# Two of twenty-four weight slices per pair of expert blocks multiplied unsplit in a mixture-of-experts layer on one Trainium2 core

## What is computed

```python
def expert_block(args):
    xe, e = args
    gu = xe @ w_gu[e] + b_gu[e]
    gate = jnp.minimum(gu[..., 0::2], SWIGLU_LIMIT)
    up = jnp.clip(gu[..., 1::2], -SWIGLU_LIMIT, SWIGLU_LIMIT)
    act = (up + 1.0) * (gate * jax.nn.sigmoid(gate * SWIGLU_ALPHA))
    return act @ w_dn[e] + b_dn[e]
```

## Time and profile before

| | |
|---|---|
| median of 3 runs | 1439.85 us |
| the three runs | 1437.68, 1439.9, 1439.85 us |
| profiled execution, its own time | 1438.17 us |
| its span in the trace | 1436.5 us |
| mean granted TensorE clock | 0.989 of full |
| DMA moved | 472.82 MB, mean 329 GB/s |

### The profile page before, as it was taken

How to read it: one execution, slowest core, us unless ns; L and a number is a source line. 1 busy time by engine, 2 the same in 40 slices (tenths; PEclk the granted TensorE clock), 3 DMA queues, 4 the chain that set the end, 5 groups by cost and what they waited for, 6 DMA issues and landing times.

```text
span 1436.5 us, 20084 instructions
## 1 busy us (share of the span) xinstructions
PE 1333.8 (93%) x6418; PEld 1058.0 (74%) x6418; DVE 1282.2 (89%) x1252; ACT 1029.2 (72%) x941; POOL 426.8 (30%) x282
## 2 busy tenths in 40 slices
PE   6999989889999999999999899999999999999996
PEld 5876866776777777777877777777777777788883
DVE  7348565789999999999999999999999999999998
ACT  5344444537788888878787888888887878877772
POOL 0000000024343536243443335343535434311100
PEclk9999999899999999999999999999999999999998
DMA  9411130279999999999999999999999999999994
GB/s 353 159 60 59 34 147 16 77 262 385 398 399 401 400 390 398 406 392 403 400 406 394 397 394 398 394 391 405 399 400 397 404 394 395 391 378 377 368 371 178
DMA packets 102341, 472.82 MB, mean 329 GB/s; under 512 B 16499, under 2 KB 16539, under 8 KB 68000
## 3 DMA queue, kind: packets, MB, share of 16 engines
q1 hardware_dynamic: 87632, 451.79, 79.6%
q0 software_dynamic: 14672, 20.53, 4.1%
HBM read 467.78 MB, written 22.02 MB: 341 GB/s over the span
## 4 chain that ended last, share of the span: by engine, by line
PE 44%; DVE 24%; issue 14%; DMA 9%; ACT 8%; DVEq 0%; SPq 0%; ACTq 0%
DVE w_lo L991 13%; PE gu_bank L1529 9%; PE gu_bank L1531 9%; PE gu_bank L1530 9%; DMA raw<-in_w_down_dram 8%; ACT w_hi L639 6%; DVE arena L1373 2%; PE turn_bank L1529 2%; PE turn_bank L1531 2%; PE turn_bank L1530 2%; PE bank L1529 2%; DVE arena L1383 1%; ACT turned L815 1%; PE bank L1531 1%; PE bank L1530 1%
## 5 line engine op out<-in xcount | busy, mean ns | idle before, releaser
L991 DVE TENSOR_TENSOR w_lo<-raw,w_hi 128x2048 fp32r<-128x2048 f32 x411 | 921.5, 2284 | 69.6 <-ACT w_hi L639 68.6
L639 ACT ACTIVATE w_hi<-raw 128x2048 fp32r<-128x2048 f32 x411 | 776.4, 1919 | 131.7 <-PE gu_bank L1531 98.9
L601 POOL DMA_INDIRECT expert_rows<-arena x32 | 222.4, 6949 | 331.4 <-ACT arena L840 172.3
L1529 PE MATMUL gu_bank<-w_hi,turned 128*128 128x512 f32 x632 | 251.9, 399 | 12.3 <-DVE w_lo L991 8.3
L1531 PE MATMUL gu_bank<-w_hi,turned 128*128 128x512 f32 x632 | 247.0, 391 | 0.0
L1530 PE MATMUL gu_bank<-w_lo,turned 128*128 128x512 f32 x632 | 247.0, 391 | 0.0
L1535 PE MATMUL gu_bank<-w_hi,turned 128*128 128x512 f32 x448 | 179.9, 402 | 29.6 <-DVE w_lo L991 28.2
L1536 PE MATMUL gu_bank<-w_lo,turned 128*128 128x512 f32 x448 | 175.1, 391 | 0.0
L1529 PEld LDWEIGHTS gu_bank<-w_hi,turned 128*128 128x128 f32 x632 | 119.0, 188 | 47.6 <-DVE w_lo L991 16.9
L1531 PEld LDWEIGHTS gu_bank<-w_hi,turned 128*128 128x128 f32 x632 | 119.0, 188 | 25.4
L1530 PEld LDWEIGHTS gu_bank<-w_lo,turned 128*128 128x128 f32 x632 | 119.1, 188 | 23.2
(11 more groups left out here) (339 smaller groups left out, 1766.6 us busy)
## 6 DMA issues: line engine op xcount, KB each, us to landing
raw<-in_w_gate_up_dram SPq DMA_DIRECT2D x264, 1024.0 KB, 11.2
raw<-in_w_down_dram SPq DMA_DIRECT2D x132, 1024.0 KB, 9.1
raw<-in_w_in_dram SPq DMA_DIRECT2D x10, 1024.0 KB, 8.3
raw<-in_w_out_dram SPq DMA_DIRECT2D x4, 1024.0 KB, 6.1
raw<-expert_rows SPq DMA_DIRECT2D x4, 1024.0 KB, 6.6
raw<-in_w_mem_kv_dram SPq DMA_DIRECT2D x2, 1024.0 KB, 12.3
arena<-in_x_dram SPq DMA_DIRECT2D x1, 2048.0 KB, 13.8
arena<-in_position_tables_dram SPq DMA_DIRECT2D x1, 2048.0 KB, 17.5
```

The costliest lines, as they stand in the source:

```text
L601: pool.indirect_dma_start(y_dram, bass.IndirectOffsetOnAxis(idx_scatter, 0), y_row, None, bounds_check=TOPK * S - 1, oob_is_err=False).the ...
L639: a.activation(home, raw_ap, ACT.Copy).then_inc(hi_ready, 1)
L991: v.tensor_tensor(home[1], raw_ap, home[0].bitcast(F32), ALU.subtract).then_inc(lo_ready, 1)
L1529: pe.matmul(bank, a[0], b[0], start=first, stop=False)
```

## The change

In each of the 14 pairs two slices are no longer split: slice 5 of gate_up of the wide block behind a narrow one, and slice 0 of the down product of the wide block, which PE does in the following narrow block's section. Both are loaded to a buffer of their own (`spare`) and multiplied as plain float32, four matmuls each, with unsplit copies of the rows or activations that ACT keeps (`keep_x`, `keep_act`). They have no `hi` and no `lo`; the counts of the slice before are raised by two. SP signals the slot they would have had (`skip_slot`). The load of the down slice stands two places earlier in SP's order, behind k5 of the narrow block; that of the gate_up slice two places later, behind k7 of the wide block.

Slices 4 to 7 of block 0 are multiplied in plain float32 too, directly from the raw slots, and have no `hi` or `lo`; the rows for them are one unsplit copy by ACT (`x_first`), and turn_x(1) of block 0 is gone from DVE. The low part of the first half of block 0's rows is made on DVE after L1275 instead of after L1296.

The biases are loaded, split and saved during the projections (on DVE before lo_a(7)), the first block takes its bias rows from DRAM as the others do, and ones and the shifted identity are built by ACT. The last two slices before the attention ends are split two steps earlier on ACT, and on DVE at the start of a step. The loads of the final gain and the down biases move on POOL from the start of the blocks to after block 29's step.

The core of the diff (SP, PE, and the order on ACT and DVE in a pair):

```diff
+            def skip_slot(i, free):
+
+                sp.wait_ge(lo_ready, free)
+                sp.sem_inc(raw_in[i % 6], 16)
...
+            def narrow_after_wide(b, first=False):
+
+                before, e = experts_of(b)
+                for k in range(GU):
+                    if first and 2 <= k < 2 + GU - FIRST_WHOLE:
+                        sp.wait_ge(half_used, 19 + k)
+                    gate_up(e, k, GU + k, b * 12 + (7 + k))
+                    if k == 5:
+                        sp.wait_ge(half_used, b * 12 + 6)
+                        sp.dma_start(spare.rearrange("p (k n) -> p k n", k=2),
+                                     dn_dram[bass.ds(before, 1), :, 2 * WHOLE_DN:2 * WHOLE_DN + 2, :]
+                                     .rearrange("e p k n -> p (e k) n")).then_inc(whole_dn_in, 16)
+                for j in range(DN):
+                    if j == WHOLE_DN:
+                        skip_slot(2 * GU + j, b * 12 + (7 + GU + j))
+                    else:
+                        down(before, j, 2 * GU + j, b * 12 + (7 + GU + j))
+
+            def wide_after_narrow(b):
+
+                before, e = experts_of(b)
+                for k in range(GU):
+                    if k == WHOLE_GU:
+                        skip_slot(GU + k, b * 12 + (7 + k))
+                    else:
+                        gate_up(e, k, GU + k, b * 12 + (7 + k))
+                sp.wait_ge(half_used, b * 12 + (1 + GU + WHOLE_DN))
+                sp.dma_start(spare.rearrange("p (e n) -> p e n", e=1),
+                             gu_dram[bass.ds(e, 1), :, WHOLE_GU, :].rearrange("e p n -> p e n")).then_inc(whole_gu_in, 16)
+                for j in range(DN):
+                    down(before, j, 2 * GU + j, b * 12 + (7 + GU + j))
...
+            def gate_up_whole(n):
+
+                pe.wait_ge(whole_gu_in, n * 16)
+                for c in range(4):
+                    ins = pe.matmul(psum[c], x_whole, spare[:, c * 512:(c + 1) * 512], start=False, stop=False)
+                ins.then_inc(half_used, 1)
+
+            def down_whole(n):
+
+                pe.wait_ge(whole_dn_in, n * 16)
+                for kk in range(2):
+                    for c in range(2):
+                        at0 = kk * D + c * 512
+                        ins = pe.matmul(psum[4 + c], act_whole[:, kk * P:(kk + 1) * P], spare[:, at0:at0 + 512],
+                                        start=kk == 0, stop=False)
+                ins.then_inc(half_used, 1)
...
-                for i in range(4, 7):
-                    lo_m(GU + i, b)
+                lo_m(GU + 4, b, 2)
+                lo_m(GU + 6, b)
...
-                for i in range(7, 12):
+                lo_m(GU + 7, b, 2)
+                for i in range(9, 12):
                     lo_m(GU + i, b)
...
-            turn_x(0, 1, ha, la)
             number_blocks()
             for i in (1, 2, 3):
                 lane_compare(i)
             v.wait_ge(xtp_done, 1)
             lane_compare(0)
-            turn_x(1, 2, ha, la)
             lo_m(2)
-            lo_m(3)
-            choose(pick, pick_ready, slice(0, 1))
+            lo_m(3, halves=1 + GU - FIRST_WHOLE)
             read_table()
-            for i in range(4, GU):
-                lo_m(i)
-            split_biases()
             lo_m(GU)
+            lo_m(GU + 1)
```

## The result

The changed kernel takes 1454.57 us (median; 1453.87 to 1455.21, 4 runs) against 1438.87 us of the kernel before (1437.68 to 1439.9, 4 runs). The ratio is 1.0108, with a 95% interval of 1.0096 to 1.0121: slower by 15.7 us, where 11.5 more (1450) had been forecast. The profiled execution has a span of 1452.7 us, 16.2 more than before.

A forecast was written before the change was run, and what follows sets the result against it. PE was taken to bound a pair's wide part, DVE its narrow part, with the DMA nearly full. From 1438.17 us, startup -3.5, products +10.8 and load order +4.2 gave +11.5: 1449.7, said as 1450, range 1434 to 1461.

The forecast's parts named there:

- The sign and its reason: Slower, chance 0.72: DVE and ACT savings fall beside a busy PE in the wide part of each pair.
- CA: Part of a pair with the wide down product, then wide gate_up; PE's, mean 36.91 us, forecast to become 37.68.
- The term of the products: Wide part of 14 pairs: two f32 slices add 1.44 us, closed gaps return 0.67; +0.77 each, +10.8 us.
- The term of the load order: Narrow gate_up: early down load makes k6 and k7 land later; 0.3 us a pair, bounds 0 and 1.3; +4.2 us.
- B: Part of a pair with the narrow block's gate_up behind the narrow down product; 28.93 us, DVE without a break.
- The startup: Everything before the pairs: forecast 3.5 us earlier at mark 350.17, bounds -1 and -9.
- the third edit: In the attention, two early slices' copies two steps sooner: -1 us, bounds -2.5 and +0.5.
- first narrow mark: First row transpose after the first narrow block's gate_up; 350.17 before, forecast near 346.7, wrong before 344 or after 350.
- The DVE lag at the wide mark: Rival: clamps 1.1 us after the wide block's row transpose come in time; 1434.7 us; faster by first or last rival 0.16.
- The full price of the order: Rival: the load order costs its full 1.3 us per pair, +18.2 instead of +4.2; 1463.7 us, chance 0.12.
- The rival that the stream covers all: Gaps in the wide part were landings, or startup gained 9: 1440 us, in part 1436 to 1443; 1437 to 1443 has 0.12.
- the pairs' span: Time from first narrow mark to the wide block's mark at the pairs' end: forecast 892.9 + 15 = 908 us.

The follow-up runs named there:

- early load: Changed kernel with both slices of each pair split again, but the wide down slice 0 still loaded behind narrow k5 into its own buffer: 1445.05 us.
- half products: Changed kernel with two of the four f32 matmuls of each unsplit slice left out, products incomplete, loads unchanged: 1454.44 us, ratio 1.0115.
- the down load late: Changed kernel with two of four f32 matmuls per unsplit slice left out and the down slice's load behind narrow k7: 1454.29 us.
- both loads in place: Changed kernel, two of four f32 matmuls per unsplit slice left out, down slice loaded behind narrow k7, gate_up slice between k4 and k6: 1447.27 us.

## Why the prediction was right, and where it was off

**The sign and its reason.** Right, by the reason given: the savings on DVE and ACT lie where PE sets the pace. That was shown with one slice alone: the gate_up slice adds 0.73 us to CA, though it has 2.28 us less subtraction in it. The size, 16 us where 11.5 were forecast, is nearer than its terms: they are off by up to 4.5 us in both directions.

**The term of the products** (+10.8) measured 6.9. The price of a slice was right to 0.01 us. What was mis-sized is PE's own work in CA, which I took as 36.24, the length less the bracket of 0.33 in the earlier trace rows. The bracket counts idle time from the modelled end of the matmul before it. From start to start that gap is 0.72 us where the pitch is 0.23, and the first pitch behind it is 0.1 longer than usual, 0.59 in all (the rows around 562.94 of the earlier trace rows):

```profile
562.22 0.39 PE L1531 MATMUL gu_bank<-w_hi,turned 128*128 128x512 f32 x1
...
563.27 0.39 PE L1530 MATMUL gu_bank<-w_lo,turned 128*128 128x512 f32 x1
```

PE's work is 35.98, and 35.98 + 1.43 is 37.41, against 37.37 to 37.40 measured. The gaps to be filled were 0.93 a pair and not 0.67. Two runs with both slices of CA split bear this out: their shortest CA are 35.93 (narrow gate_up slice unsplit) and 36.01 (early load).

**The term of the load order** (+4.2, 0.3 a pair between 0 and 1.3) measured 0.67 a pair and 8.7 in all. The mechanism, its slice (narrow k6) and its chain were right; it was run by itself, with the f32 products away, and taken away by itself. Mis-sized was what takes it back: I credited the share of 0.75 in the window 528 to 530 and a longer CA that lets the stream catch up. The second hardly came: the down slice alone has B at 29.74 behind a CA of 36.70, both slices have it at 29.61 behind 37.40, so 0.70 us more of CA took 0.13 out of B. Why no more is not shown; the hole that the later gate_up load makes in CA, which I had only counted as pushing later loads, is one candidate.

**The startup** (-3.5) measured -0.35. The step that failed is the third edit, put at -1 between -2.5 and +0.5: the attention put back gives 1.74 us at the mark (2.97 with the pairs split), so the edit costs 1.7 or more, outside its bounds. I had looked at the copy's earlier start and not at DVE's queue: the subtraction moved ahead of the softmax work of its step, waits 1.51 us for its copy, and everything behind it waits with it. The rest of the startup, -2.5 in the sum, is -2.1 by the same run (348.08 against 350.17). The first narrow mark, 349.82, is just inside the 350 from which the forecast was to count as wrong, and far from its 346.7.

**The rivals.** The DVE lag at the wide mark did not go: B never fell below 28.92 with DVE relieved only in CA. The full price of the order did not come either. The rival that the stream covers all was half true in a way that the forecast did not have: the stream is a second limit at the changed kernel's pair length, so that with the loads in this order even half of the f32 products left the time at 1454 us. The errors offset in part: products 3.9 too high, order 4.5 too low, the startup's gain 3.1 too large, and 0.9 behind the pairs. That the pairs' span was forecast at 908 us and measured at 908.5 is luck: the first two errors cancel in it.

**What the Trainium skill gave.** The four passes of true FP32 (Trainium skill, "FP8 and Floating Point Precision", TensorE Precision Notes), taken at the trace's pitch of 0.2264 us, give an estimate of 3.62 us a slice; 3.43 was measured. The ceiling of 435 GB/s (Trainium skill, "DMA: Bandwidth & Descriptors", Where 436 GB/s comes from) is not what a pair gets: at shares of 0.99 to 1.02 the windows of a CA or a B above carry 394 to 410.

## What to carry to other kernels

Before work is taken off one engine, cut the loop at marks and ask of each part which engine has no idle time in it: a saving in a part that another engine fills is worth only that engine's gaps, and those are read from start to start, not from the idle brackets. In an in-order queue a load whose buffer is free waits behind one whose slot is not, and a load put early is paid by the next one that lands late. When two limits of equal length hold a loop, relieving one shows nothing; take work out altogether, as the half products did, and see whether the time moves. Look at the granted clock of each trip of the loop before two traces are compared: here it alone made 0.9 us that looked like a gap, and clouded one experiment.

## What the runs showed of the hardware

In f32 a matmul of 512 columns against 128 x 128 costs 0.86 us as two records of 0.43, an f32r one 0.23, so four f32 matmuls in place of twelve f32r ones cost 0.71 us more, and in place of eight 1.62.

At the granted clock of 0.50 f32r matmuls of this shape are 0.43 us apart instead of 0.23 (changed kernel, 1270.49 to 1270.92).

In the pairs of the kernel before and of the changed one the granted clock stays full. With the half products it falls to 0.50 in three pairs, with the down load late in five (6.8 us each time), and with both loads in place in five (3.4 us each). Every one of these falls comes behind a wait of PE of 1.8 to 2.0 us; the pairs of the kernel before and of the changed one hold no wait that long. Not every such wait is followed by a fall: of the two gaps of block 29, 2.15 us before and 2.14 in the changed kernel, only the second is. So a kernel made lighter on PE can lose some of the time again to the clock: 0.4 to 0.6 us in each pair it falls in where both loads are in place, none with the half products alone, where landings hold the pair.
